# Sixteen more tokens on fetched rows in a PEER stage, with a third gate piece and picks ordered by rank

## What is computed

```python
def peer(xn, w_q, sub_keys, u, v):
    q = (xt @ w_q).reshape(T, PEER_HEADS, 2, PEER_HALF)
    s = jnp.einsum('thpc,hpnc->thpn', q, sub_keys)          # 128 keys each
    s1, i1 = lax.top_k(s[:, :, 0], PEER_TOPK)
    s2, i2 = lax.top_k(s[:, :, 1], PEER_TOPK)
    cand = (s1[..., :, None] + s2[..., None, :])            # 16 x 16 pairs
    top_s, top_j = lax.top_k(cand, PEER_TOPK)
    expert = ...                                            # i1 * 128 + i2 of the 16 best
    gate = jax.nn.softmax(top_s, axis=-1)
    h = gelu(einsum('cd,chkd->chk', xc, u[expert]))
    out = einsum('chk,chkd->cd', gate * h, v[expert])
```

## Time and profile before

| | us |
|---|---|
| median of 3 executions | 3197.86 |
| lowest, highest | 3192.72, 3202.19 |
| the profiled execution, its own time | 3196.02 |
| its span, first to last instruction | 3194.2 |
| PE busy | 3147.9 |
| DVE busy | 2544.4 |
| ACT busy | 1633.9 |
| POOL busy | 1021.8 |

### The profile page before, as it was taken

One profiled execution on the slowest core, in us unless ns is written; L12 is line 12 of the kernel. 1 busy time (PEld: TensorE's weight loads), 2 busy tenths in 40 slices (PEclk: granted clock), 3 DMA queues, 4 the chain that ended last, 5 costly groups with the idle time before them and its releaser, 6 DMA issues.

```text
span 3194.2 us, 48684 instructions
## 1 busy us (share of the span) xinstructions
PE 3147.9 (99%) x17786; PEld 2816.8 (88%) x17786; DVE 2544.4 (80%) x5378; ACT 1633.9 (51%) x3053; POOL 1021.8 (32%) x626
## 2 busy tenths in 40 slices
PE   8999999999999999999999989999999999999999
PEld 7878899999998888888978868899999998888887
DVE  5685898989867888885378876898989866888886
ACT  5343249696943333335355654248686863333333
POOL 1001364545422444430000001364445432444440
PEclk9999999999999999999999999999999999999999
DMA  5113269898999999994222214259898998999994
GB/s 192 47 59 120 85 214 352 307 354 304 349 368 333 380 393 392 393 370 126 68 86 74 87 61 139 80 178 344 314 346 313 333 373 322 372 401 396 393 389 147
DMA packets 324925, 827.06 MB, mean 259 GB/s; under 512 B 26064, under 2 KB 158672, under 8 KB 317520
## 3 DMA queue, kind: packets, MB, share of 16 engines
q1 hardware_dynamic: 250960, 555.48, 48.5%
q0 software_dynamic: 73728, 268.47, 22.5%
HBM read 717.89 MB, written 105.96 MB: 258 GB/s over the span
## 4 chain that ended last, share of the span: by engine, by line
PE 44%; DVE 3%; DMA 2%; ACT 1%; issue 1%; SPq 0%; ACTq 0%; DVEq 0%
PE p_bank L2356 16%; PE p1r_h_ps L2292 16%; PE ba_bank L420 6%; PE o_bank L1763 1%; DMA raw<-in_u 1%; PE p1r_gate_ps L2340 1%; PE ba_oT_ps L482 1%; PE ba_t_ps L504 1%; PE p1r_s_ps L2316 0%; PE ba_s_ps L443 0%; ACT p1r_cols L2462 0%; DVE p_grow L2721 0%; PE ba_s_ps L449 0%; PE ba_o_ps L494 0%; DMA hiddens<-p_h_sb 0%
## 5 line engine op out<-in xcount | busy, mean ns | idle before, releaser
L2423 ACT ACTIVATE peer_hi<-raw 128x1024 fp32r<-128x1024 f32 x540 | 571.0, 1057 | 666.2 <-PE p_bank L2356 612.8
L2713 DVE TENSOR_TENSOR peer_lo<-raw,peer_hi 128x1024 fp32r<-128x1024 f32 x434 | 530.4, 1224 | 310.3 <-ACT peer_hi L2423 289.5
L2254 POOL TENSOR_TENSOR peer_lo<-raw,peer_hi 128x1024 fp32r<-128x1024 f32 x106 | 263.6, 2488 | 1079.0 <-ACT peer_hi L2423 1079.0
L2266 POOL DMA_INDIRECT p_grow<-in_v_rows,p_expert x256 | 386.7, 1511 | 470.9 <-DVE p_acc L2730 385.3
L2266 POOL DMA_INDIRECT p_grow<-in_u_rows,p_expert x256 | 361.7, 1413 | 508.0 <-DVE p_hid L2721 478.6
L2356 PE MATMUL p_bank<-peer_hi,p_w_lo 128*128 128x512 f32 x1500 | 461.9, 389 | 0.0
L2356 PE MATMUL p_bank<-peer_hi,p_w_hi 128*128 128x512 f32 x1500 | 461.7, 389 | 0.0
L2356 PE MATMUL p_bank<-peer_lo,p_w_hi 128*128 128x512 f32 x1500 | 461.7, 389 | 0.0
L2292 PE MATMUL p1r_h_ps<-h_hi,peer_hi 128*128 128x384 f32 (+2 forms) x1152 | 397.5, 345 | 1.5 <-ACT p_h_sb L2441 1.0
L2292 PE MATMUL p0r_h_ps<-h_hi,peer_hi 128*128 128x384 f32 (+2 forms) x1152 | 396.8, 344 | 0.8 <-ACT p_h_sb L2441 0.5
L2292 PE MATMUL p1r_h_ps<-h_lo,peer_hi 128*128 128x384 f32 (+2 forms) x1152 | 391.8, 340 | 0.0
(11 more groups left out here) (438 smaller groups left out, 5525.7 us busy)
## 6 DMA issues: line engine op xcount, KB each, us to landing
raw<-in_u SPq DMA_DIRECT2D x256, 512.0 KB
raw<-in_v SPq DMA_DIRECT2D x256, 512.0 KB
p_g_sb<-gates SPq DMA_DIRECT2D x64, 768.0 KB
hiddens<-p_h_sb SPq DMA_DIRECT2D x240, 192.0 KB
p_w_raw<-hiddens SPq DMA_DIRECT2D x60, 768.0 KB
gates<-x SPq DMA_DIRECT2D x24, 1024.0 KB
raw<-in_w_b_mix SPq DMA_DIRECT2D x38, 512.0 KB, 3.5
raw<-in_w_peer_q SPq DMA_DIRECT2D x32, 512.0 KB, 4.3
```

What stands on the lines that cost most here:

```text
L2254: pool.tensor_tensor(lo[:, m % NH, :], raw[:, m % NR, :], hi[:, m % NH, :].bitcast(F32), ALU.subtract).then_inc(lo_pool, 1)
L2266: pool.indirect_dma_start(out=grow[:, g % RG, :], out_offset=None, in_=table, in_offset=bass.IndirectOffsetOnAxis(ap=expert[:, at:at + 1], ...
L2423: act.activation(hi[:, n % NH, :], raw[:, n % NR, :], ACT.Copy).then_inc(hi_ready, 1)
L2713: dve.tensor_tensor(lo[:, m % NH, :], raw[:, m % NR, :], hi[:, m % NH, :].bitcast(F32), ALU.subtract).then_inc(lo_dve, 1)
```

## The change

Sixteen tokens (0 to 15 of tile 1) leave the dense `u` products. Their 16 x 128 rows of `u` are fetched as 16 more fetches of 128 rows (8 partitions per token, 16 picks each), multiplied with a prepared copy of the 16 tokens (`xfew`), and their gelu times the gate is the finished weight. In the dense way a constant 1 stands where their hiddens would, and the weight is placed in their gate's stead, as a sum of three bf16 pieces and not of two f16 pieces, because it has no bound that would let it be scaled. The two batches of these tokens are placed last, so the placing order and the steps of the routes shift. Four small round trips through DRAM spread and gather the 16 tokens' values: `few_x` (512 KB each way), names and gates (`few`), weights (`few_w`). Within a route everything is ordered rank, head where it was head, rank; eight multiplies become one.

```diff
+    NE = 16
+    SPREAD = P // NE
+    NJ = PAIRS // SPREAD
+    FEW0 = PART
+    ROWS_ALL = 2 * PAIRS + NJ
+    PLACE_ORDER = [*range(4, BATCHES), 2, 3, 0, 1]
+    FIRST_PLACED = [0, 0, TILE_BATCHES - 4, 2 * TILE_BATCHES - 4]
...
-    route_step = [LIST_END, LIST_END + 8, LIST_END + 41, LIST_END + 74]
+    route_step = [LIST_END, LIST_END + 8, LIST_END + 35, LIST_END + 68]
...
         if any(s <= n <= turns_after(t) for t, s in enumerate(route_step)):
-            return 4
+            return 6
         if n < WEIGH0:
-            return 14
+            return 16
         return 7 if n < FRONT + 4 * CH else 13
...
+    FEW_NAMED = turns_after(1)
+    FEW_SUMMED = rows_step(FEW0 + NJ)
+    FEW_TURN = FEW_SUMMED + 13
...
-                sp.dma_start(g_dram[:, b, at, :], gbuf[b % 2][:, at, :]).then_inc(g_stored[b % 2], 16)
+                sp.dma_start(g_dram[:, (b + 1) % NTD, at, :], gbuf[b % 2][:, at, :]).then_inc(g_stored[b % 2], 16)
...
+                if n == 2:
+                    store_few_x()
+                if n == 4:
+                    load_few_x()
+                if n == FEW_NAMED:
+                    store_few()
+                if n == FEW_NAMED + 2:
+                    load_few()
+                if n == FEW_SUMMED + 8:
+                    store_few_w()
+                if n == FEW_SUMMED + 10:
+                    load_few_w()
...
+                if g == 1:
+
+                    pool.wait_ge(few_x_stored, 16)
+                if g == FEW0:
+                    pool.wait_ge(few_indexed, 1)
...
-                first = 0 if n < NQ else P
+                first = 0 if n < NQ else P + NE
...
+            def turn_few():
+                pe.wait_ge(few_w_loaded, 16)
+                pe.transpose(t_ps[:, 3 * P:3 * P + NE], few_row[0:NE, :], ident[0:NE, 0:NE]).then_inc(few_turned, 1)
...
+                    if is_few(k):
+                        for c in range(PIECES + 1):
+                            piece = cols_of(k, c) if c < PIECES else third[:, k % 2, :, :, :]
+                            mm = pe.matmul(gate_ps[:, q % 2, v % GROUP, :], rows_of_batch(k)[:, v // 2, :, v % 2],
+                                           piece[:, v // 2, :, v % 2], start=c == 0, stop=c == PIECES)
...
-                act.activation(h_sb[:, j % 2, :], h_ps[:, n % 2, P:S], ACT.Gelu).then_inc(taken, 1)
+                else:
+                    unit(h_sb[:, j % 2, 0:NE])
+                act.activation(h_sb[:, j % 2, NE:SD], h_ps[:, n % 2, P + NE:S], ACT.Gelu).then_inc(taken, 1)
...
                 for s in range(2):
...
-                    for a in range(HEADS):
-                        mine = hit[:, :, a * TOPK:(a + 1) * TOPK].rearrange("p c (k b) -> p c k b", b=2)
-                        step.mark(dve.tensor_tensor(
-                            mine, mine, best_b[:, 2 * a + s, :, :].unsqueeze(2).broadcast_to([P, TOPK, TOPK // 2, 2]),
-                            ALU.mult))
-                    step.wait()
+                    mine = hit.rearrange("p c (k h) -> p c k h", h=HEADS)
+                    step(dve.tensor_tensor(
+                        mine, mine, best_c[:, s, :, :].unsqueeze(2).broadcast_to([P, TOPK, TOPK, HEADS]), ALU.mult))
...
+            def cut_few():
+
+                dve.wait_ge(few_turned, 1)
+                dve.wait_ge(done, 1)
+                weights = t_ps[:, 3 * P:3 * P + NE]
+                dve.tensor_copy(few_head[:, :], weights).then_inc(few_cut, 1)
+                dve.wait_ge(few_cut, 1)
+                dve.tensor_copy(piece0[:, 0:NE], few_head[:, :]).then_inc(few_cut, 1)
+                dve.tensor_tensor(few_rest[:, :], weights, few_head[:, :], ALU.subtract).then_inc(few_cut, 1)
+                dve.wait_ge(few_cut, 3)
+                dve.tensor_copy(few_tail[:, 0, :], few_rest[:, :]).then_inc(few_cut, 1)
+                dve.wait_ge(few_cut, 4)
+                dve.tensor_tensor(few_tail[:, 1, :], few_rest[:, :], few_tail[:, 0, :], ALU.subtract).then_inc(few_cut, 1)
...
+                if is_few(k):
+                    dve.tensor_tensor(cols_of(k, 1), same_of(k), per_token(few_tail[:, 0, :], k), ALU.mult)
+                    dve.tensor_tensor(third[:, k % 2, :, :, :], same_of(k), per_token(few_tail[:, 1, :], k),
+                                      ALU.mult).then_inc(cols_ready, 1)
...
+                if kind == "few":
+                    if at == 0:
+                        dve.wait_ge(few_x_loaded, 16)
+                    dve.tensor_tensor_reduce(row, row, xfew[:, :], 1.0, 0.0, ALU.mult, ALU.add,
+                                             few_hid[:, at:at + 1]).then_inc(used, 1)
+                    return
...
+            dve.scalar_tensor_tensor(out=grow[0:NE, 1, :], in0=x[0:NE, 1, :], scalar=rstd[0:NE, 1:2],
+                                     in1=grow[0:NE, 0, :], op0=ALU.mult, op1=ALU.mult).then_inc(xrow_ready, 1)
```

More of the change, by code:

```diff
@@ L2014, in cut_step, with placed_tile, is_few @@
         return turns_after(t) + 1
+    def placed_tile(k):
+        return max(t for t in range(1, TT) if k >= FIRST_PLACED[t])
+    def is_few(k):
+        return PLACE_ORDER[k] * BATCH < NE
     def hot_step(k):
-        return cut_step(1 + k // TILE_BATCHES) + (k % TILE_BATCHES) * 7 // 5
+        t = placed_tile(k)
+        return cut_step(t) + (k - FIRST_PLACED[t]) * 7 // 5
     def place_block(k):
@@ L2047, in taken_rows, with row_of, hidden_rows @@
     def taken_rows(n):
-        return min(2 * PAIRS, row_sums[n] // 10)
+        return min(ROWS_ALL, row_sums[n] // 10)
+    def row_of(g):
+        if g < FEW0:
+            return "u", g
+        if g < FEW0 + NJ:
+            return "few", g - FEW0
+        if g < PAIRS + NJ:
+            return "u", g - NJ
+        return "v", g - NJ - PAIRS
+    def hidden_rows(i):
+        return PART * (i + 1) + (NJ if PART * (i + 1) > FEW0 else 0)
     def fetched(n):
@@ L2106, in peer_stage @@
             index_f = early.sb("index_f", [P, HK])
-            shifted = early.sb("shifted", [P, HEADS, TOPK])
-            gate = early.sb("gate", [P, HEADS, TOPK])
+            shifted = early.sb("shifted", [P, TOPK, HEADS])
+            gate = early.sb("gate", [P, TOPK, HEADS])
             gsum = early.sb("gsum", [P, HEADS])
+            xfew = early.sb("xfew", [P, D])
+            few = early.sb("few", [P, 2, NJ])
+            few_expert = early.sb("few_expert", [P, NJ], U32)
+            few_hid = early.sb("few_hid", [P, NJ])
+            few_act = early.sb("few_act", [P, NJ])
+            few_w = early.sb("few_w", [P, NJ])
+            few_row = early.sb("few_row", [P, HK])
+            few_head = early.sb("few_head", [P, NE], BF16)
+            few_rest = early.sb("few_rest", [P, NE])
+            few_tail = early.sb("few_tail", [P, 2, NE], BF16)
+            third = table[:, 0:BATCH * NK].bitcast(BF16).rearrange("p (s a j b) -> p s a j b", s=2, j=NK, b=2)
             idle = early.sb("idle", [P, 1])
@@ L2169, in x_half_done, with same_of, rows_of_batch, cols_of @@
             return 2 if t == 0 else 2 * t + c + 1
+        def same_of(k):
+            t = same[:, :, :, :]
+            return t.bitcast(BF16) if is_few(k) else t
+        def rows_of_batch(k):
+            t = rows[:, k % 2, :, :, :]
+            return t.bitcast(BF16) if is_few(k) else t
+        def cols_of(k, c):
+            t = cols[:, k % 2, c, :, :, :]
+            return t.bitcast(BF16) if is_few(k) else t
         def wait_lo(eng, n):
@@ L2212, in load_gates, with store_few_x, load_few_x, store_few @@
                     .then_inc(g_loaded[c % 2], 16)
+            def store_few_x():
+                sp.wait_ge(xrow_ready, 2)
+                sp.dma_start(few_x_dram, grow[0:NE, 1, :].unsqueeze(1).broadcast_to([NE, SPREAD, D]))\
+                    .then_inc(few_x_stored, 16)
+            def load_few_x():
+                sp.wait_ge(few_x_stored, 16)
+                sp.dma_start(xfew[:, :], few_x_dram.rearrange("t q d -> (t q) d")).then_inc(few_x_loaded, 16)
+            def store_few():
+                sp.wait_ge(few_named, 1)
+                sp.dma_start(few_dram[:, 0, :], index_f[0:NE, :]).then_inc(few_stored, 16)
+                sp.wait_ge(routed, 1)
+                sp.dma_start(few_dram[:, 1, :], gate[0:NE, :, :].rearrange("p k h -> p (k h)"))\
+                    .then_inc(few_stored, 16)
+            def load_few():
+                sp.wait_ge(few_stored, 32)
+                for a in range(2):
+                    sp.dma_start(few[:, a, :], few_dram[:, a, :].rearrange("t (q j) -> t q j", j=NJ))\
+                        .then_inc(few_loaded, 16)
+            def store_few_w():
+                sp.wait_ge(few_weighed, 1)
+                sp.dma_start(few_w_dram, few_w[:, :]).then_inc(few_w_stored, 16)
+            def load_few_w():
+                sp.wait_ge(few_w_stored, 16)
+                sp.dma_start(few_row[0:NE, :], few_w_dram.rearrange("(t q) j -> t (q j)", q=SPREAD))\
+                    .then_inc(few_w_loaded, 16)
```

(14 more changed lines are left out.)

136 lines of the change are left out of this document (89 added, 47 removed).

## The result

The changed kernel takes 3217.25 us (median of 4; 3212.85 to 3219.87), the kernel before on the same chip 3195.29 (3190.01 to 3202.19): ratio 1.0074, with a 95% interval of 1.0060 to 1.0089. It is slower by some 22 us, where I had forecast some 23 us faster (the terms of my sum: −41.0 + 2.1 + 5.7 + 10). The profiled execution of the changed kernel took 3212.85 us for its span of 3211.1, against 3196.02 and 3194.2.

A forecast was written before the change was run, and what follows sets the result against it. PE, paid by the column, was taken to bound the u products: 3196.0 − 41.0 + 1.9 + 0.2 + 5.7 + 10 = 3172.8, stated as 3175 us (−0.7%) by the median. The range was 3157 to 3192.

The forecast's parts named there:

- Columns, −41.0: u products: 368 columns in place of 384 save 6.67 ns a matmul on PE, 41.0 us over two layers.
- third piece and transpose, +2.1: On PE: 16 more matmuls a layer for the third weight piece, +1.9 us, and their transpose, +0.2 us.
- Rival D: u products: fewer columns buy nothing because weight loads set the pace, 3200 us; chance 2%.
- The picks' multiply at 1.15 us: Route, on DVE: one multiply of 2048 elements replaces eight of 256 taking 1.71 us, −0.56 us each, twice a route.
- SP's new waits at nothing: SP's queue: the new waits lie behind events already past, so they cost nothing and do not hold raw loads.
- Route ends, +5.7: DVE's first lower half late for PE: 6.6 us in both layers less 0.9 now; bounds 0 and 3 us each.
- Rival B: DVE no longer keeps up in routes, six ends cost 20 us, or the multiply runs at half pace: 3189 us; 13%.
- Placing, +10: While gates are placed, PE's stalls of some 8 us double and a bit, +10 us; bounds −5 and +30.
- the check of 382 GB/s asked against 391 sustained: Placing: traffic scaled by bytes and time needs 382 GB/s; v products sustain 391, so it fits by 2%.
- Rival A: Every cover holds, no more stalls than now: 3157 us, 3159 by the median; chance 12%.
- Rival C: Placing: the DMA's ceiling with this traffic is what it moves now, 350 GB/s, so slower, 3215 us; chance 9%.
- four signs by which I said I would be wrong: Block over 4.1 us; placing below 360 GB/s, ACT awaiting raw; PE idle over 30 us in u; PE awaiting new semaphores.

The follow-up runs named there:

- the columns alone: Kernel before with u products cut to 368 columns and nothing else, a constant 1 for the 16 tokens' hiddens, no added rows: 3174.8 us, ratio 0.9941.
- the pace alone: Kernel before with the same 256 rows fetched earlier, 0.6 a block in routes and 1.6 between (0.4 and 1.4 before): 3216.93 us, ratio 1.0075.
- the load first: SP issues the next raw block's load ahead of the last block's store of hiddens: changed kernel 3200.71 us, kernel before 3186.46 us.
- the old pace between the routes: Changed kernel with 1.4 fetched rows a block between routes in place of 1.6, 0.6 kept inside, the rest in the v products: 3190.62 us, ratio 0.9994.
- half of the gates' bytes: Changed kernel without storing the second half of each gates tile, its first half loaded instead, so results are incomplete: 3179.17 us, ratio 0.9958.
- the old paces and SP's load first: Changed kernel with 0.4 rows a block in routes and 1.4 between, and SP's next raw load ahead of the store of hiddens: 3159.18 us, ratio 0.9888.

## Why the prediction was wrong

Two steps failed, one at the route ends and one in the placing; the other terms held. Point by point:

- **What bounds the kernel:** right. PE is paid by the column: 167.5 ns at 368 columns.
- **Columns, −41.0, third piece and transpose, +2.1:** right as far as the trace separates them; with them the balance closes to 1.6 us. Rival D is out.
- **The picks' multiply at 1.15 us:** right. It takes 1.23 us alone and 3.3 behind POOL.
- **SP's new waits at nothing:** right by the traces, which show 3.2 us of SP's waiting for `index_f` and 1.5 for the small weights in layer 1. Raw loads were late for another reason.
- **Route ends, +5.7:** wrong, +25.0. The step that failed is "DVE's last comparison cannot start before POOL's last subtraction ends", with everything counted from there. In the kernel before the comparison was on when POOL ended, and the count from there came out. With blocks 0.16 us shorter DVE falls a whole subtraction behind POOL and reaches that comparison 1.7 us after POOL has ended. At all six route ends the timelines say the same: before, it starts 2.2 to 2.4 us ahead of POOL's end, and in the changed kernel 1.0 to 2.9 us behind it. With the columns alone it is 0.5 to 2.2 us behind, with the pace alone 2.2 to 3.0 ahead. So the shorter blocks make the lag, and the pace puts more rows behind the comparison (two at every end of the changed kernel, one at the first two ends of a layer before). I had counted the two rows behind the comparison and not the lag in front of it. I wrote that waits for POOL could take up one more row ahead of the comparison; they could not. A reading failed with it: that a row's product "keeps its 1.23 us" beside POOL. The product in those rows came after POOL's last subtraction and shows nothing of the kind. In the kernel before, two of 256 products, each started early in one of POOL's subtractions, took 2.9 and 3.0 us. In the changed kernel nine did, all in the second and third routes, and took 3.3 to 3.4 us. So a row inside a route can cost DVE 3.3 us, and not 1.23. The bound of 3 us a route end did not hold either: 26.1/6 is 4.4 us, of which the waits for the gate and for the lower half are 16.3/6 = 2.7 and most of the rest is the slow clock behind them (7.5 us in the six blocks that came late). Rival B had this step ("every route end costs 3 to 4 us"), at 13%.
- **Placing, +10:** wrong, +32.4, a little beyond my bound of +30. The step that failed is the check of 382 GB/s asked against 391 sustained, by which the traffic fitted. The average rate was not what decided. With the load first the changed kernel kept PE at 69.77 of 70 us with 364 GB/s, so 382 was not even asked there; and with the columns alone, where the same bytes pass in blocks 4% shorter, the stalls doubled. What decided is when a load is issued and when it must have landed, and bytes and rows count by how they shift the two: the old pace between the routes took 22 us of placing stalls away, half of the gates' bytes 38, the order 14. The load shown above had 13.4 us from its issue until ACT was free for it, and took 15.3; and SP issues it behind a store that waits for ACT. With the load first the kernel before lost its last placing stall. I read the one burst of layer 1 as bad luck that might double. It was a loop near its edge, ACT to SP to DMA to ACT, and both the columns (+8.9) and the pace (+12.0) pushed it; the whole change costs 32.4, more than their sum.
- **Rival A**, every cover holds: 3159 us, as forecast for it, is what the change takes with the old paces and SP's load first (3159.18). So the 41 us are there; the pace and the order spent them. That the two numbers agree to the us is luck: some 19 us of stalls are still in that kernel, 9 more than before, and its profiled execution took 3164.4.
- **Rival C**, the slower one: its time (3215) is near the measured one and its mechanism did not happen. A ceiling near 350 GB/s would hold in every block of placing; but stalls come singly, and 364 GB/s passed with PE at 69.77 of 70 us. The `v` products do show a limit of the DMA: over the 305 us in which rows are fetched all the time, at 1.5 rows a block PE waits while 409 GB/s are moved, and at 1.4 and 404 it does not (the kernel with the old pace between the routes alone):

```profile
2735.00:3040.00 305.00, 305.00 (x1347) 252.57 (x1346) 277.18 (x258) 108.88 (x114) 165.04 (x105) 1.00 1.04 404
```

The 358 GB/s of HBM bandwidth a core that the Trainium skill gives (DMA: Bandwidth & Descriptors, the opening table) are exceeded by all of these.

Of the four signs by which I said I would be wrong, two appeared: placing below 360 GB/s with ACT waiting for raw blocks, and PE losing over 30 us in the `u` products.

The range of 3157 to 3192 was too narrow because it took both stalls as separate, small and bounded by what one event had cost. Both were edges: 0.6 us to spare at the route ends, and a load that is late by 2 us as soon as the DMA has a burst.

What stays open: whether a third buffer for hiddens would remove the rest of the placing stalls, which now begin at that buffer (not tried), and why blocks shorter by 0.16 us put DVE a whole subtraction behind. With both old paces and the load first 9.4 of the 10.9 us called placing lie in blocks 130 to 135, behind the last placed batch. There SP waits up to 2.8 us for the last store of gates and issues loads of gates of 768 KB between the raw loads, and a store of hiddens took 14.1 us to leave its buffer. So a second rival for the rest is the place of these loads of gates, which was not tried either.

## What to carry to other kernels

Before making the bounding engine faster, list every producer that is in time by less than the time saved per step times the steps to its deadline: here a route end had 0.6 us to spare, and blocks shorter by 0.16 us were enough, without any added work, to make the six route ends 15 us late. Work that is "hidden" has a place as well as an amount: taking some 17 rows a layer in the `u` products and not in the `v` products cost 42 us there, and the `v` products took them for nothing at 1.4 a block. So move a schedule's side work to where the slack is, in the same change. And where one queue issues in program order, put loads that have a deadline ahead of stores that wait for a consumer.

## What the runs showed of the hardware that was not expected

- A stall of PE costs more than its wait. Behind layer 1's first route the granted clock was 0.89 over 10 us, 0.83 behind the stall in placing. At the six route ends of the changed kernel 16.3 us of waits became 26.1 us of lost time.
- The same comparison takes 1.24 or 3.3 us, by whether it meets POOL's subtraction, and so does a fetched row's product: 1.22 us in the median, 3.31 where POOL had begun 0.2 us before it. The changed kernel, layer 1's third route, POOL then DVE:

```profile
2437.05 2.45 POOL L2358 TENSOR_TENSOR peer_lo<-raw,peer_hi 128x1024 fp32r<-128x1024 f32 x1 [0.84 <-ACT peer_hi L2545]
```
```profile
2437.27 3.31 DVE L2903 CUSTOM_DVE_ANT_0 p_grow<-p_grow,p_xrow 128x1024 f32<-128x1024 f32 x1
```

Behind POOL's last subtraction no op is stretched any more, so DVE's lag arrives there in full.
- One core moved 403 GB/s over 400 us of `v` products with PE full (the kernel with the old pace between the routes alone):

```profile
2700.00:3100.00 400.00, 400.00 (x1767) 331.20 (x1766) 358.89 (x341) 141.23 (x147) 207.46 (x132) 1.00 1.04 403
```
